# Gelus, the last expert rows and the norm between two layers, arranged anew

## What is computed

```python
# hb: 256 tokens x 1024, normed
q = (hb @ w_q).reshape(n, 8, 2, 128)             # query projection, 2048 columns
s = jnp.einsum('nhid,hikd->nhik', q, sub_keys)   # 128 scores per head and half
...                                              # 16 best of the 16 x 16 sums, idx
w = jax.nn.softmax(best, axis=-1)
act = jax.nn.gelu(jnp.einsum('nhkd,nd->nhk', jnp.take(u_tab, idx, axis=0), hb))
out = jnp.einsum('nhk,nhkd->nd', w * act, jnp.take(v_tab, idx, axis=0))
...
h = rmsnorm(h + out, ln_final_w)                 # final norm of the first block
u = rms_norm(h, ret_norm_pre)                    # norm ahead of the retention layer
q, k, v, g = jnp.split(u @ ret_w_in, ...)        # 1024, 1024, 2048, 2048 columns
q = rope(q, pos); k = rope(k, pos) * 256 ** -0.5 # x1*cos - x2*sin, x1*sin + x2*cos
```

## Time and profile before

| | us |
|---|---|
| median of 3 runs | 1671.98 (1670.53 to 1674.44) |
| profiled execution | 1673.2 |
| its span | 1671.4 |
| busy PE / DVE / ACT / POOL | 1438.1 / 1102.5 / 701.4 / 305.1 |
| bytes moved | 415.37 MB, of which the gathers 268.45 MB |

### The profile page before, as it was taken

One profiled execution on the slowest core, in us unless ns is written; L12 is line 12 of the kernel. 1 busy time (PEld: TensorE's weight loads), 2 busy tenths in 40 slices (PEclk: granted clock), 3 DMA queues, 4 the chain that ended last, 5 costly groups with the idle time before them and its releaser, 6 DMA issues.

```text
span 1671.4 us, 19357 instructions
## 1 busy us (share of the span) xinstructions
PE 1438.1 (86%) x6773; PEld 1010.1 (60%) x6773; DVE 1102.5 (66%) x2088; ACT 701.4 (42%) x1203; POOL 305.1 (18%) x260
## 2 busy tenths in 40 slices
PE   6998998999898798778777777777789999799987
PEld 6986796776887733333333333333388688788866
DVE  6765478786667858677777777765476456654554
ACT  5664464345455432222222222221344465566853
POOL 0000000000002246445544444443100000000000
PEclk9999999999999889999998999999889999899989
DMA  6552353343465899999999999999635456454432
GB/s 218 159 145 89 92 161 101 99 128 116 142 223 206 322 416 421 422 421 422 422 421 422 421 422 421 422 422 421 261 120 165 138 172 193 131 169 141 152 116 86
DMA packets 77855, 415.37 MB, mean 249 GB/s; under 512 B 9008, under 2 KB 9008, under 8 KB 44736
## 3 DMA queue, kind: packets, MB, share of 16 engines
q0 software_dynamic: 36864, 268.45, 38.7%
...
## 4 chain that ended last, share of the span: by engine, by line
PE 28%; DMA 24%; DVE 6%; ACT 3%; issue 1%; POOL 1%; DVEq 0%; ACTq 0%; POOLq 0%
PE ps L247 20%; DMA AR<-in_peer_uv,C 13%; DMA SLAB<-in_peer_uv,C 12%; PE ps L306 8%; DVE AR L1141 1%; DVE SLAB L1141 1%; PE ps L309 1%; POOL SLAB L1132 0%; POOL AR L1132 0%; ACT whi L208 0%; ACT AR L953 0%; ACT AR L1163 0%; DVE AR L1061 0%; DVE AR L1064 0%; DVE AR L1062 0%
## 5 line engine op out<-in xcount | busy, mean ns | idle before, releaser
L306 PE MATMUL ps<-AR 128*128 128x512 f32 (+7 forms) x1396 | 411.2, 442 | 121.3 <-ACT AR L1163 69.0
L209 DVE TENSOR_TENSOR wlo<-raw,whi 128x1024 fp32r<-128x1024 f32 x257 | 312.7, 1222 | 171.4 <-ACT whi L208 168.8
L306 PEld LDWEIGHTS ps<-AR 128*128 128x128 f32 (+3 forms) x1396 | 204.9, 185 | 308.8 <-issue 145.7
L208 ACT ACTIVATE whi<-raw 128x1024 fp32r<-128x1024 f32 x257 | 269.4, 1054 | 124.6 <-PE ps L247 117.7
L306 PE MATMUL ps<-SLAB,AR 128*128 128x512 f32 x516 | 254.7, 650 | 67.3 <-ACT AR L1163 67.2
L247 PE MATMUL ps<-XH,whi 128*128 128x256 f32 (+1 forms) x1032 | 305.9, 296 | 5.4 <-DVE XL L317 4.3
L247 PE MATMUL ps<-XH,wlo 128*128 128x256 f32 (+1 forms) x1032 | 297.6, 288 | 0.0
L247 PE MATMUL ps<-XL,whi 128*128 128x256 f32 (+1 forms) x1032 | 297.6, 288 | 0.0
L1132 POOL DMA_INDIRECT AR<-in_peer_uv,C x127 | 152.1, 1197 | 677.1 <-DVE C L1086 525.8
L306 PEld LDWEIGHTS ps<-SLAB,AR 128*128 128x128 f32 x516 | 105.0, 208 | 215.2 <-issue 124.0
L247 PEld LDWEIGHTS ps<-XH,whi 128*128 128x128 f32 x1032 | 201.4, 195 | 24.0 <-issue 14.9
...
## 6 DMA issues: line engine op xcount, KB each, us to landing
raw<-in_stream SPq DMA_DIRECT2D x257, 512.0 KB, 3.7
...
AR<-in_rows SPq DMA_DIRECT2D x4, 512.0 KB, 5.0
...
AR<-in_xin SPq DMA_DIRECT2D x2, 512.0 KB, 5.1
...
```

Of the source, the lines that this page charges most:

```text
L208: a = A(lambda e: e.activation(h[:, :], r, ACT.Copy), loaded[i], free, chain=False)
L209: b = V(lambda e: e.tensor_tensor(l[:, :], r, h[:, :].bitcast(F32), ALU.subtract), a, loaded[i], free, chain=False)
L306: return PE(lambda e: e.matmul(out_ap, l, r, start=start, stop=stop, skip_group_check=onto), *after, signal=sig)
```

## The change

- **Gelus.** Until the last scores are in, dots gather in one group of up to 16 rows (broken at multiples of 16, where the tile changes) with no gelu; the side work takes one more empty step first. Afterwards groups of 4.
- **Last rows.** Groups of 2 from row 244 on and of 1 from row 254 on, each weighed at once, not one step later. `LAST_WIDE` is 240, but from there on only the first 10 slots take gathers, so that `XL`'s part is free too. The five splits stand at rows 245 to 249, and the weight loads behind them wait until the last gather has landed (`hold`).
- **Rows turned unnormalized.** `finish_tile(i)` adds a tile's banks to H and turns the sums with plain transposes (printed at line 309), the product of both gains (`gain`) put in as the scale of the split into `XH`/`XL`; squares come behind. Tile 0 is done in steps between rows 244 to 249, tile 1 after row 255.
- **Norm.** PE takes the q and k chunks with unnormalized rows. `tables()`, behind the second chunk, spreads the norm over the partitions (ones times diagonals, into bank 6) and multiplies it into cosine and sine (CS, 256 KB, loaded with gfin near row 223); the copies of v and g out of PSUM have the norm as their scale. K2 is loaded as before, but first read later.

```diff
@@ -25,12 +25,12 @@
 ARENA = 27648
-LAST_WIDE = 234
+LAST_WIDE = 240
 NEG = -3.0e38
...
 P_LNMIX, P_BGATE, P_GLAN, P_CONVW, P_CONVB, P_DTB, P_ALOG, P_SSDN = 0, 8, 12, 14, 110, 134, 135, 136
-P_RPRE, P_KVN, P_SBN, P_FFN, P_GATE2 = 152, 160, 168, 176, 184
+P_RPRE, P_KVN, P_SBN, P_FFN, P_FIN, P_GATE2 = 152, 160, 168, 176, 184, 192
 NPAR = P_GATE2 + 512
@@ -192,12 +192,12 @@
         loaded, split, used = {}, {}, {}
-        state = {"load": 0, "split": 0, "next": 0, "limit": PEER_END, "fence": None}
+        state = {"load": 0, "split": 0, "next": 0, "limit": PEER_END, "fence": None, "hold": None}
...
                 state["load"] += 1
-                loaded[i] = dma(SP, raw[i % NR][:, :], stream[i], s_raw[i % NR], split.get(i - NR))
+                loaded[i] = dma(SP, raw[i % NR][:, :], stream[i], s_raw[i % NR], split.get(i - NR), state["hold"])
@@ -1115,7 +1115,7 @@
-            names = [j for j in range(len(slots)) if (m < LAST_WIDE or not TILES <= j < TILES + NS) and slot_free(j)]
+            names = [j for j in range(len(slots) if m < LAST_WIDE else TILES) if slot_free(j)]
             return min(names, key=lambda j: holds.get(j, -1)) if names else None
@@ -1186,56 +1186,81 @@
             gathers()
-            yield
-            yield
-            yield
+            for _ in range(4):
+                yield
+            group = []
             for m in range(256):
                 dot(m)
-                size = 2 if m < 24 else 4
-                while len(waiting) > 0 and "st7" in pts:
+                group.append(m)
+                while waiting and "st7" in pts:
                     weighed()
-                if m % size == size - 1:
-                    ms = list(range(m - size + 1, m + 1))
-                    gelu(ms)
-                    waiting.append(ms)
+                size = 16 if "st7" not in pts else 4 if m < 244 else 2 if m < 254 else 1
+                if len(group) >= size or m % 16 == 15:
+                    gelu(group)
+                    waiting.append(group)
+                    group = []
+                    while waiting and m >= 244:
+                        weighed()
                 gathers()
...
                         ahead = topk(n_ahead) if n_ahead < 16 else iter(())
-                if m >= LAST_WIDE + 6 and m % 2 == 0:
+                if n_ahead == 16 and "cs" not in pts:
+                    pts["cs"] = dma(SP, CS, con2[:, E_COS:E_COS + 512], s_cs, pts["st7"])
+                    pts["gfin"] = dma(SP, gfin, rows[0:1, B_FIN:B_FIN + 1024].broadcast_to([128, 1024]), s_rows, idx_pt[15])
+                    pts["gain"] = V(lambda e: e.tensor_tensor(SM[:, 32:40], par_(P_FIN, 8), par_(P_RPRE, 8), ALU.mult))
+                if 255 in uv_in and m >= LAST_WIDE + 4:
                     if state["fence"] is None:
                         state["fence"] = read[max(x for x, j in slot_of.items() if TILES <= j < TILES + NS)]
-                        state["limit"] = len(chunks)
+                        state["limit"], state["hold"] = len(chunks), uv_in[255]
                     if state["split"] < PEER_END + NS:
                         do_split(state["split"])
-                yield
-            while waiting:
-                weighed()
-            yield
+                if m == LAST_WIDE + 4:
+                    tile0 = finish_tile(0)
+                if m >= LAST_WIDE + 4:
+                    next(tile0, None)
+                yield
+            yield
+
+        gfin = place("gfin", 8192, 1024)
+        J = place("J", 9216, 512)
+        CS = place("CS", 13824, 512)
+        s_cs = sem("s_cs")
+        rp = {}
+
+        def finish_tile(i):
+
+            cols = slice(128 * i, 128 * i + 128)
+            low = read[max(x for x, j in slot_of.items() if j >= TILES + NS)]
+            hs, added = [H[:, i, 512 * half:512 * half + 512] for half in range(2)], {}
+            for half, hh in enumerate(hs):
+                added[half] = bank_free[2 * i + half] = V(
+                    lambda e, hh=hh, b=2 * i + half: e.tensor_tensor(hh, hh, ps[b][:, :], ALU.add), pts[f"ffn{i}"])
+            for k in range(8):
+                b = 4 + k % 4 if i == 0 or k < 4 else k - 4
+                t = tr(ps[b][:, 0:128], H[:, i, 128 * k:128 * k + 128], True, added[k // 4], bank_free[b])
+                rp[k, i] = bank_free[b] = split_to(lambda X, k=k: X[:, TX * k:TX * k + TX][:, cols], ps[b][:, 0:128],
+                                                   SM[:, 32 + k:33 + k], t, low, pts["gain"])
+                if k % 2:
+                    yield
+            for half, hh in enumerate(hs):
+                square(hh, i, half, added[half], base=16, scratch=J)
+            for half, hh in enumerate(hs):
+                hg = HN[:, i, 512 * half:512 * half + 512]
+                v = V(lambda e, hh=hh, hg=hg, half=half: e.tensor_tensor(hg, hh, gfin[:, 512 * half:512 * half + 512], ALU.mult),
+                      pts["gfin"])
+                square(hg, i, half, v, base=20, scratch=J)
...
         side_all()
-        A(lambda e: e.activation(SM[:, 30:31], SM[:, 30:31], ACT.Sqrt))
-
-        gfin = place("gfin", 8192, 1024)
-        J = place("J", 9216, 512)
-        gr_in = dma(SP, gfin, rows[0:1, B_FIN:B_FIN + 1024].broadcast_to([128, 1024]), s_rows, idx_pt[15])
-        for i in range(2):
-            hs = [H[:, i, 512 * half:512 * half + 512] for half in range(2)]
-            for half, hh in enumerate(hs):
-                v = bank_free[2 * i + half] = V(lambda e, hh=hh, b=2 * i + half: e.tensor_tensor(hh, hh, ps[b][:, :], ALU.add),
-                                                pts[f"ffn{i}"])
-                square(hh, i, half, v, base=16, scratch=J)
-            for half, hh in enumerate(hs):
-                hg = HN[:, i, 512 * half:512 * half + 512]
-                v = V(lambda e, hh=hh, hg=hg, half=half: e.tensor_tensor(hg, hh, gfin[:, 512 * half:512 * half + 512], ALU.mult), gr_in)
-                square(hg, i, half, v, base=20, scratch=J)
-        ring.update(banks=(0, 1, 2, 3), steps=1)
-        peer_done = (v, pts["ffn0"], pts["ffn1"])
+        for _ in finish_tile(1):
+            pass
+        ring.update(banks=(4, 5, 7), steps=1)
+        peer_done = (V.now(), pts["ffn0"], pts["ffn1"])
         K2 = place("K2", 2048, NC2)
@@ -1248,7 +1273,7 @@
         rstd(both, None, 4)
-        V(lambda e: e.tensor_tensor(rr, SM[:, 16:18], r2, ALU.mult))
+        rr_done = V(lambda e: e.tensor_tensor(rr, SM[:, 16:18], r2, ALU.mult))
@@ -1268,9 +1293,20 @@
-        xr, = features(HN, rr, [P_RPRE], [0], peer_done)
-        for i in range(2):
-            hf = V(lambda e, i=i: e.scalar_tensor_tensor(H[:, i, :], H[:, i, :], SM[:, 16 + i:17 + i], gfin, ALU.mult, ALU.mult))
+        def tables():
+
+            v = diagonals(DN, rr)
+            ones = V(lambda e: e.memset(J[:, 0:128], 1.0), sq)
+            for i in range(2):
+                t = mm(ps[6][:, 128 * i:128 * i + 128], J[:, 0:128], DN[:, i, :], True, True, i == 1, v, ones, bank_free[6])
+            for j in range(2):
+                v = pts["tables"] = bank_free[6] = V(lambda e, j=j: e.tensor_tensor(CS[:, 256 * j:256 * j + 256], CS[:, 256 * j:256 * j + 256],
+                                                                                   ps[6][:, 0:256], ALU.mult), t, pts["cs"])
+            for i in range(2):
+                pts["hf"] = V(lambda e, i=i: e.scalar_tensor_tensor(H[:, i, :], H[:, i, :], SM[:, 16 + i:17 + i], gfin, ALU.mult,
+                                                                    ALU.mult))
+
+        xr = {k: (rp[k, 0], rp[k, 1]) for k in range(8)}
         QR = place("QR", 4608, 4096).rearrange("p (f t) -> p f t", f=16)
@@ -1278,7 +1314,7 @@
         SC = place("SC", 22528, 768).rearrange("p (b c) -> p b c", b=2)
-        cos, sin = K2[:, E_COS:E_COS + 256], K2[:, E_SIN:E_SIN + 256]
+        cos, sin = CS[:, 0:256], CS[:, 256:512]
         rope_free = {}
@@ -1286,9 +1322,11 @@
                 if f % 2:
+                    if f == 1:
+                        tables()
                     x1, x2, t = RX[:, j - 1, :], RX[:, j, :], RX[:, 4, :]
                     y1, y2 = QR[:, f - 1, :], QR[:, f, :]
-                    V(lambda e: e.tensor_tensor(t, x2, sin, ALU.mult), a, k2_in)
+                    V(lambda e: e.tensor_tensor(t, x2, sin, ALU.mult), a)
                     V(lambda e: e.tensor_tensor(y1, x1, cos, ALU.mult))
@@ -1298,6 +1336,7 @@
         stream_T([(0, TX, cons_rope(f)) for f in range(16)], 0, TX, xr)
+        ring["banks"] = (0, 1, 2, 3)
@@ -1369,20 +1408,27 @@
-        def use_v(blk, tt, o, tok):
-            a = A(lambda e: e.copy(VN[:, tt, 512 * blk:512 * blk + 512], o), tok, ret.get("free"))
+        def use_v(blk, tt, o, tok, scale=1.0):
+            a = A(lambda e: e.activation(VN[:, tt, 512 * blk:512 * blk + 512], o, ACT.Copy, scale=scale), tok)
             if tt:
...
-        def use_sg(blk, tt, o, tok):
```

(12 more changed lines are left out.)

3 lines of the change are left out of this document (2 added, 1 removed).

## The result

Over 20 runs of each, the changed kernel takes 1678.26 us in the median (1674.70 to 1686.26) and the kernel before 1673.46 (1670.07 to 1682.57). The ratio is 1.0029, 95% interval 1.0017 to 1.0042: **4.9 us slower, between 2.8 and 7.0**. The forecast was 2.8 slower, in a range of 9 faster to 9 slower around the profiled run.

A forecast was written before the change was run, and what follows sets the result against it. The prediction took the expert phase to be bound by DMA, its gathers moving 421 GB/s. Start -6.0, tail +13.2 and transition -4.4 summed to +2.8 us: 1674.8, rounded 1675 us, range 1664 to 1682.

The forecast's parts named there:

- Term 1: Query projection: ending 16 us earlier frees gather slots, so DMA has 2.6 gathers less left; -6.0 us, bounds -1.9 and -9.
- rival D: Query projection: PE waits for splits behind late dots instead, so the start brings only -2; 1679 us, chance 0.15.
- The tail: Last expert rows: tile 0's transposes in DVE's and ACT's queues wait for PE; +13.2 us, bounds +5 and +17.
- rival A: Last rows: DVE keeps up to row 249, only the held weight chunk stops it; -8.3 us, 1664, chance 0.18.
- the ring: Last rows: dots wait behind tile 0's low parts, these for PE's transposes; 12.3 us per pair, where landing gives 5.0.
- Term 2: Between the experts and the next matrix: PE starts on unnormalized rows, then stands for the norm; -4.4 us, bounds -9 and 0.
- Norm in the later PSUM copies: Later copies out of PSUM: the same instructions with a scale; zero.
- Rival C: Clock: all bursts of two and chunks 0 to 2 run at half rate; +5, 1680 us, chance 0.07.
- the transition: The stretch from the experts' end into the next matrix, forecast as Term 2: -4.4 us.

The follow-up runs named there:

- e1: The kernel before with only the new gelu-free grouping in the query projection; ratio 0.9970 to the kernel before.
- e4: The changed kernel with the norm and cosine/sine table products behind the fourth chunk instead of the second; ratio 0.9997 to the kernel before.
- e3: The changed kernel with tile 0 finished behind row 255, just ahead of tile 1; ratio 1.0042 to the kernel before.
- e2: The changed kernel without the hold on weight loads; ratio 1.0028 to the kernel before.

## Why the prediction was right

**Term 1, -6.0.** The step was that 16 us of earlier slots are worth 2.6 gathers. The start alone brought 6.1 at the experts' end and 5.0 in the time, and the bytes moved ahead of the first freed slot were 2.7 gathers' worth more. The projection's last copy came at 47.7 behind the anchor; forecast were 46.0, and with PE's waits at 0.62 us at most rival D is out. The experts started 65.4 behind it (forecast 65.8). With gfin's and the tables' 0.79 MB ahead of it, row 240 came 4.3 us earlier; forecast 4.1. The tables are not loaded near row 223, though, where the instruction stands in the program: the load waits for the last scores alone and goes out at 565.96, gfin's at 1106.93. For the sum both stand ahead of row 240, and it makes no difference. That the term held came from counting bytes and not waits of PE.

**The tail, +13.2.** The mechanism was right. In the profiled execution the tail costs 9.9 us against e1; in e4, whose last rows are the same program, 13.1. Counted from the dot of row 244:

| | forecast | after | the same rows in e4 |
|---|---|---|---|
| dot 245 | 11.5 | 10.4 | 10.5 |
| dot 247 | 23.8 | 20.9 | 23.9 |
| dot 249 | 37.5 | 34.6 | 38.0 |
| end of the fifth split | 42.5 | 39.3 | 42.8 |
| PE ends the experts | 56.5 | 53.5 | 57.1 |

The 3 us between the two executions are there by dot 247 and stay. They are one burst of two rows: the sum took it cold (5.2 us), after ran it warm (3.7), e4 at the low clock (6.6). PE's rows in e4, beside those of the changed kernel above:

```profile
1172.99 3.78 PE L306 MATMUL ps<-AR 128*128 128x512 f32 x4 [3.33 <-ACT AR L1163]
1176.56 3.08 PE L306 MATMUL ps<-SLAB,AR 128*128 128x512 f32 x4
```

The last eight rows ran at 2.1 us each in both, and not at 1.78. Start and tail together are +3.9 at the experts' end in the profiled execution and +7.1 with e4's, where +7.2 were forecast. Here the check named beforehand decided: dot 249 at 37 us (34.6 and 38.0 came), within 20 us if rival A held. The last row landed about where forecast: the held load went out 677.8 us behind the anchor, and 676.6 were forecast.

**Rival A**, that the tail hides and only the held chunk stops it, was wrong for this kernel, but its mechanism was there: with tile 0 out of the way it set the end (e3). I had it as an alternative to the ring; it was a second stop behind it.

**Term 2, -4.4.** Measured are 57.0 us and not 60.0 from the experts' end to the last q/k chunk: -3.0. The products of the tables were forecast 13.0 us behind the experts' end and came at 13.3, but PE stood 4.4 us ahead of them and not 3. The sum put the cold stretch behind the stand at 1.7 us; 13 us at a granted clock of 0.74 are 3.4 (an estimate, 0.26 of 13 us), and these 1.7 more are about the 1.4 that the term missed. The timeline shows where the chain came from, the split between the norm and the diagonals:

```profile
1230.41 1.23 DVE L209 TENSOR_TENSOR wlo<-raw,whi 128x1024 fp32r<-128x1024 f32 x1 [0.46 <-ACT whi L208]
1231.67 0.29 DVE L321 TENSOR_SCALAR AR<-C,SM 128x128 f32<-128x128 f32 x1
```

**Norm in the later PSUM copies, zero.** While v and g run, PE waits five times for ACT, 0.87 us each instead of 0.77, 0.5 us in all. From the last q/k copy to the end the profiled run takes 2.7 us more than before. That I can't settle: e1, whose program behind that point is that of before, takes 2.5 more too, and the runs with the new copies take 398.7 to 400.9 us there, before 398.2. So no effect can be told from zero here.

**The sum.** Forecast +2.8; at the last q/k copy the traces show +0.9, by two errors of opposite sign (the tail 3.3 less, the transition 1.4 more), while the medians say +4.9 (2.8 to 7.0). The run without the hold, in effect the same kernel, has +3.2 at that point; at the end of the span the two have +3.6 and +5.9. With e4's tail instead (+7.1) and the transition's -3.0 the sum would be +4.1. The sign was carried by the tail, and that the experiments confirm; the closeness of 2.8 to 4.9 is partly luck, since the transition was overrated and the clock moves the tail by 3 us from one execution to the next.

**The clock.** In the changed kernel PE ran rows 244 and 245 behind an idle of 3.33 us at the full clock, and the next two behind 6.34 us not (windows of both, then of the eight last rows):

```profile
1178.50:1182.10 3.60, 3.57 (x9) 1.61 (x10) 1.23 (x1) 1.22 (x2) 1.00 (x1) 1.00 1.01 428
1189.00:1195.20 6.20, 6.19 (x9) 2.56 (x10) 1.23 (x1) 1.20 (x2) 0.00 (x0) 0.57 0.10 44
1202.70:1219.30 16.60, 16.55 (x32) 6.92 (x32) 8.73 (x17) 4.62 (x12) 0.00 (x0) 0.84 0.12 34
```

A clock of 1.00 is the level of 2.4 GHz, and 0.57 is nearly all of it at 1.2. Behind the very same 3.33 us, rows 244 and 245 had 0.68 in e2 and 0.55 in e4:

```profile
1175.70:1181.10 5.40, 5.39 (x10) 2.38 (x11) 1.22 (x1) 1.19 (x2) 0.94 (x1) 0.68 1.01 426
1172.90:1179.60 6.70, 6.61 (x10) 2.79 (x11) 1.23 (x1) 1.27 (x3) 0.94 (x1) 0.55 0.99 418
```

So the pair took 3.7, 5.4 and 6.6 us behind one and the same idle. The Trainium skill, "TensorE: Matmul & The Clock Gate", section "Loop structure matters more than you think", has matmuls run cold behind a long wait: here that held behind 6.3 and 7.2 us in all three executions, and behind 3.3 in two of three. Rival C had every pair slow and 5 us more for it. But the sum had counted its pairs cold already (5.2 us in the round of 12.3), so that a large part of C's price was in the forecast; in e4 both pairs were slow, and the experts' end came at 57.1, where the forecast had 56.5. In after it was the pair behind 6.34 us (6.3 us and not 3.6) and a part of the last eight rows (16.6 and not 14.2 at 1.78 each), 5.1 us together.
